# The value convolution and the low weight parts on GpSimd, and a reciprocal and square root in place of a logarithm and exponential, in the first projection stage of a two-block kernel

## What is computed

```python
r, k, v, wd, ad, gd = cols                       # columns of the projection x @ w_in
r, k, v = split(conv_fn(concatenate([r, k, v])), 3)   # depthwise 3x3 on the grid, 1x3 in the context
kk = heads(k * k_k)
kk = kk / maximum(sqrt(sum(kk * kk, per head)), 1e-12)
for d in range(2):
    w = -softplus(-(w0[d] + tanh(wl) @ w2[d])) - 0.5
    a_flat = sigmoid(a0[d] + al @ a2[d])
    kd = heads(k * (1.0 + (a_flat - 1.0) * k_a))
    bonus.append(sum(rh * kd * r_k, per head) * vh)
```

## Time and profile before

| | before |
|---|---|
| median of 3 runs | 5515.27 us (5512.98 to 5518.95) |
| the profiled execution | 5518.95 us, of which 5517.2 us from first to last instruction |
| granted TensorE clock, mean | 0.860 |
| busy: PE, DVE, ACT, POOL | 4372.5, 2100.7, 1445.7, 863.7 us |
| first and last product of the stage `front` | 231 and 885 us |
| steps of one half | 231 to 534 us, then 577 to 885 us |

### The profile page before, as it was taken

The page is one execution under the profiler, slowest core; times in us unless marked ns, Lnnn a source line. Parts: engine busy times, 40 slices in busy tenths (PEclk is TensorE's granted clock), DMA queues, the critical chain, the costliest instruction groups (busy, mean ns, idle before and its releaser), DMA issues. The chain is left out here.

```text
span 5517.2 us, 85137 instructions
## 1 busy us (share of the span) xinstructions
PE 4372.5 (79%) x33087; PEld 2998.3 (54%) x33088; DVE 2100.7 (38%) x3440; ACT 1445.7 (26%) x2777; POOL 863.7 (16%) x836
## 2 busy tenths in 40 slices
PE   4698896777768857369999999999607999884569
PEld 0497886767667753334444444444305777663434
DVE  0288685555533341321111111111266663235600
ACT  0276564222200000202333333333102221342200
POOL 2100001333300000041111111111122333001100
PEclk9799898989955558589999999999858999996689
DMA  3444444212032323228588887322463223204331
GB/s 137 123 147 152 128 145 132 67 52 65 23 73 57 67 74 137 70 79 292 205 311 299 323 300 278 135 94 92 155 236 70 77 77 95 81 20 98 67 122 64
DMA packets 615451, 720.50 MB, mean 131 GB/s; under 512 B 89380, under 2 KB 495652, under 8 KB 615172
## 3 DMA queue, kind: packets, MB, share of 16 engines
q1 hardware_dynamic: 554184, 544.39, 31.8%
q0 software_dynamic: 39344, 135.94, 6.6%
q10 hardware_dynamic: 21648, 36.18, 1.8%
HBM read 542.44 MB, written 173.97 MB: 130 GB/s over the span
## 5 line engine op out<-in xcount | busy, mean ns | idle before, releaser
L2337 PE MATMUL routed_p_gu<-routed_wgu,routed_xT 128*128 x2048 | 903.2, 594 | 7.9 <-SPq L2261 7.5
L2337 PEld LDWEIGHTS routed_p_gu<-routed_wgu,routed_xT 128*128 128x128 f32 x2048 | 381.0, 191 | 438.2 <-issue 438.2
L2319 PE MATMUL routed_p_y<-routed_wd,routed_hT 128*128 x1024 | 460.5, 593 | 1.4 <-DVE routed_y L2386 1.4
L2357 ACT ACTIVATE routed_xT<-routed_p_x,moe_bias,moe_scale 128x128 f32<-128x128 f32 x1032 | 374.1, 468 | 99.2 <-PE routed_p_x L2308 99.2
L2398 DVE TENSOR_TENSOR routed_hid<-routed_sg,routed_p_gu 128x256 f32<-128x256 f32 x128 | 53.9, 421 | 873.9 <-ACT routed_sg L2368 873.9
L1850 PE MATMUL out_ps<-out_w,out_a 128*128 128x512 f32 x768 | 334.2, 599 | 58.4 <-DMA out_x<-h 36.4
L626 PE MATMUL front_ps<-front_a_high,front_w_high 128*128 128x320 f32 (+1 forms) x1120 | 364.2, 325 | 16.7 <-DVE front_w_low L861 13.6
L626 PE MATMUL front_ps<-front_a_high,front_w_low 128*128 128x320 f32 (+1 forms) x1120 | 355.5, 317 | 0.0
L626 PE MATMUL front_ps<-front_a_low,front_w_high 128*128 128x320 f32 (+1 forms) x1120 | 355.3, 317 | 0.0
L2319 PEld LDWEIGHTS routed_p_y<-routed_wd,routed_hT 128*128 128x128 f32 x1024 | 194.9, 190 | 245.7 <-issue 245.7
L2284 POOL DMA_INDIRECT results<-routed_y,routed_yidx x128 | 124.9, 976 | 1169.8 <-DVE routed_idx L2377 871.8
(11 more groups left out here) (509 smaller groups left out, 7431.8 us busy)
## 6 DMA issues: line engine op xcount, KB each, us to landing
routed_wgu<-in_exp_w_gate_dram SPq DMA_DIRECT2D x64, 1024.0 KB, 6.9
routed_wgu<-in_exp_w_up_dram SPq DMA_DIRECT2D x64, 1024.0 KB, 11.9
routed_wd<-in_exp_w_down_dram SPq DMA_DIRECT2D x64, 1024.0 KB, 13.9
front_wt<-in_w_in_dram SPq DMA_DIRECT2D x70, 512.0 KB, 4.3
sum_part<-results SPq DMA_DIRECT2D x8, 4096.0 KB, 13.7
mod_w<-in_w_mod_dram SPq DMA_DIRECT2D x12, 2048.0 KB, 7.7
pre_wt<-in_w_in_dram SPq DMA_DIRECT2D x44, 512.0 KB, 3.9
proj<-pre_xv SPq DMA_DIRECT2D x16, 512.0 KB, 2.6
```

Of the source, the lines that this page charges most:

```text
L2319: op = nc.tensor.matmul(p_y[:, h, :], hT[:, k, :], wd[:, bass.ds(e % WS, 1), k, h * BANK:(h + 1) * BANK], start=(k == 0), stop=(k == MT - 1))
L2337: op = nc.tensor.matmul(p_gu[:, :], xT[:, b % 2, k, :], wgu[:, bass.ds(e % WS, 1), k, :, :], start=(k == 0), stop=(k == KD - 1))
L2357: op = nc.scalar.activation(xT[:, b % 2, k, :], p_x[:, k // 4, (k % 4) * P:(k % 4 + 1) * P], ACT.Identity, bias=bias[:, 0, k:k + 1], scale ...
```

## The change

POOL takes over `low` (all 70 low parts) and the whole value convolution, tap by tap: one multiply by a scalar into `term` and one add, with a drain ahead of each. The taps of one unit are cut over the six steps v to g (2, 2, 1, 2, 1, 2 taps for n < 4 and 1, 2, 1, 2, 1, 1 for n >= 4), each time behind `low(s + 2)`. The centre taps of k and r and the affine part of kd move from ACT to DVE, that of v to POOL. The logarithm and exponential become a reciprocal on DVE and a square root on ACT. The product of kk with the root, and `keys(n, 0)`, move from step q to step v on DVE.

```diff
@@ -589,10 +587,46 @@
 
         @block.gpsimd
         def _(pool):
-            for t, (src, idx) in enumerate(sources[0] + sources[1]):
-                size = src.shape[0]
-                pool.wait_ge(scaled, t + 1)
-                nc.gpsimd.tensor_tensor(yb[0:size, t % 2], yb[0:size, t % 2], row_shift[idx][0:size], ALU.add).then_inc(y_made, 1)
+            def low(s):
+                pool.wait_ge(w_rounded, s + 1)
+                nc.gpsimd.tensor_tensor(w_low[:, s % 2], wt[:, s % 2], w_high[:, s % 2], ALU.subtract).then_inc(w_split, 1)
+
+            def value_taps(n, first, last):
+
+                t, dst = taps[:, n % QT, 2, :], b("vc")
+                steps_of = around(n)
+                if first == 0:
+                    pool.wait_ge(bonus_made, n)
+                    pool.wait_ge(v_sent, 16 * n)
+                    nc.gpsimd.tensor_scalar(dst, raw[:, 2, offset(n):offset(n) + HALF], t[:, 4:5], None, ALU.mult)
+                for where, src, k in steps_of[first:last]:
+                    pool.drain()
+                    nc.gpsimd.tensor_scalar(where(b("term")), src(raw[:, 2]), t[:, k:k + 1], None, ALU.mult)
+                    pool.drain()
+                    nc.gpsimd.tensor_tensor(where(dst), where(dst), where(b("term")), ALU.add)
+                if last >= len(steps_of):
+                    pool.drain()
+                    pool.sem_inc(v_made, 1)
+
+            for s in range(N):
+                if s in (0, PER):
+                    for j, (src, idx) in enumerate(sources[s // PER]):
+                        t, size = s // PER * NT + j, src.shape[0]
+                        pool.wait_ge(scaled, t + 1)
+                        nc.gpsimd.tensor_tensor(yb[0:size, t % 2], yb[0:size, t % 2], row_shift[idx][0:size], ALU.add).then_inc(y_made, 1)
+                        if s == 0 and j in (1, 2):
+                            low(j - 1)
+                if s == 0:
+                    pool.wait_ge(once, 16 * ONCE)
+                if s + 2 < N:
+                    pool.wait_ge(mm_done, s + 1)
+                    low(s + 2)
+                for lag in range(6):
+                    n = at(s, "v", lag)
+                    if n is not None:
+                        pool.wait_ge(evicted, s - lag + 1)
+                        cuts = (0, 2, 4, 5, 7, 8, 10) if n < QT else (0, 1, 3, 4, 6, 7, 8)
+                        value_taps(n, cuts[lag], cuts[lag + 1])
...
@@ -709,13 +743,6 @@
                 act.wait_ge(aux_ready, 7 * n + j + 1)
                 return aux[:, (7 * n + j) % 2, :, 0:HALF // 2]
 
-            def keys(n, d):
-                if n:
-                    act.wait_ge(fac_made[d], n)
-                act.drain()
-                nc.scalar.activation(b(("kd0", "kd1")[d]), b(("sa0", "sa1")[d]), ACT.Identity, scale=cols[:, n % QT, KA:KA + 1],
-                                     bias=cols[:, n % QT, OMKA:OMKA + 1]).then_inc(kd_made[d], 1)
-
             def factors(n, d):
                 act.wait_ge(logs[d], n + 1)
                 inc, exc, neg = (("cm0", "ex0", "ng0"), ("sw1", "ex1", "ng1"))[d]
@@ -756,19 +783,7 @@
                 elif kind in ("k", "r", "v"):
                     if n:
                         act.wait_ge({"k": k_made, "r": r_made, "v": v_made}[kind], n)
-                    j, dst = {"r": (0, "rc"), "k": (1, "kc"), "v": (2, "vc")}[kind]
-                    nc.scalar.copy(two(raw[:, j, :]), wide).then_inc(evicted, 1)
-                    if n:
-                        if kind == "r":
-                            act.wait_ge(fac_made[1], n)
-                        elif kind == "k":
-                            act.wait_ge(prod_made, n)
-                        else:
-                            act.wait_ge(bonus_made, n)
-                            act.wait_ge(v_sent, 16 * n)
-                    act.drain()
-                    nc.scalar.activation(b(dst), raw[:, j, offset(n):offset(n) + HALF], ACT.Copy, scale=taps[:, i, j, 4:5])\
-                        .then_inc(centred[j], 1)
+                    nc.scalar.copy(two(raw[:, {"r": 0, "k": 1, "v": 2}[kind], :]), wide).then_inc(evicted, 1)
                 elif kind == "q":
                     if n:
                         act.wait_ge(h_made[1], n)
@@ -793,14 +808,11 @@
                     if n:
                         act.wait_ge(fac_sent[0], 80 * n)
                     nc.scalar.activation(two(b("sa0")), ready, ACT.Sigmoid, bias=cols[:, i, A0:A0 + 1]).then_inc(aux_act, 1)
-                    keys(n, 0)
                     act.wait_ge(kk_made, n + 1)
                     nc.scalar.activation(b("sq"), b("kk"), ACT.Square).then_inc(kk_squared, 1)
                 elif kind == "v":
-                    act.wait_ge(aux_dve, 2 * n + 1)
-                    nc.scalar.activation(b("sq"), b("sq"), ACT.Ln)
-                    act.drain()
-                    nc.scalar.activation(b("sq"), b("sq"), ACT.Exp, scale=-0.5).then_inc(kk_rooted, 1)
+                    act.wait_ge(kk_inverse, n + 1)
+                    nc.scalar.activation(b("sq"), b("sq"), ACT.Sqrt).then_inc(kk_rooted, 1)
                 elif kind == "q":
                     ready = take(n, 3)
                     if n:
@@ -808,7 +820,6 @@
                     nc.scalar.activation(two(b("sw1")), ready, ACT.Sigmoid, bias=cols[:, i, W0 + 1:W0 + 2]).then_inc(aux_act, 1)
                 elif kind == "ff":
                     nc.scalar.activation(two(b("sa1")), take(n, 4), ACT.Sigmoid, bias=cols[:, i, A0 + 1:A0 + 2]).then_inc(aux_act, 1)
-                    keys(n, 1)
                     factors(n, 0)
                 elif kind == "fb":
                     for d in range(2):
@@ -845,8 +856,6 @@
                             dve.wait_ge(turned, t - 1)
                         nc.vector.scalar_tensor_tensor(yb[0:size, t % 2], xb[0:size, t % 2], part[:, 2:3], row_scale[idx][0:size],
                                                        ALU.mult, ALU.mult).then_inc(scaled, 1)
-                    if half == 0 and j in (1, 2):
-                        low(j - 1)
                     if j >= 1:
                         size = sources[half][j - 1][0].shape[0]
                         dve.wait_ge(high_made, t)
@@ -856,13 +865,9 @@
                             op = nc.vector.tensor_tensor(cells[0][:, h], turns[:, h], cells[1][:, h], ALU.subtract)
                         op.then_inc(low_made, 1)
 
-            def low(s):
-                dve.wait_ge(w_rounded, s + 1)
-                nc.vector.tensor_tensor(w_low[:, s % 2], wt[:, s % 2], w_high[:, s % 2], ALU.subtract).then_inc(w_split, 1)
-
             def convolution(n, j, dst):
                 t = taps[:, n % QT, j, :]
-                dve.wait_ge(centred[j], n + 1)
+                nc.vector.tensor_scalar(dst, raw[:, j, offset(n):offset(n) + HALF], t[:, 4:5], None, ALU.mult)
                 for where, src, k in around(n):
                     dve.drain()
                     op = nc.vector.scalar_tensor_tensor(where(dst), src(raw[:, j]), t[:, k:k + 1], where(dst), ALU.mult, ALU.add)
@@ -877,9 +882,12 @@
                 return by(ap, size)[:, :, k:k + 1].broadcast_to([P, n_chunks, size])
 
             def keys(n, d):
+                i = n % QT
                 kd, sa = b(("kd0", "kd1")[d]), b(("sa0", "sa1")[d])
-                dve.wait_ge(kd_made[d], n + 1)
+                dve.wait_ge(aux_act, 5 * n + (2 if d == 0 else 4))
+                nc.vector.tensor_scalar(kd, sa, cols[:, i, KA:KA + 1], cols[:, i, OMKA:OMKA + 1], ALU.mult, ALU.add)
                 nc.vector.tensor_tensor(sa, sa, b("kk"), ALU.mult)
+                dve.drain()
                 nc.vector.tensor_tensor(kd, kd, b("kc"), ALU.mult)
 
             def factors(n, d):
@@ -933,8 +941,6 @@
                     nc.vector.tensor_tensor(lb[:, :, 2, :], lb[:, :, 0, :], lb[:, :, 1, :], ALU.subtract).then_inc(lb_diff, 1)
                     dve.wait_ge(lb_sig, 1)
                     nc.vector.tensor_scalar(lb[:, :, 3, :], lb[:, :, 2, :], -1.0, 1.0, ALU.mult, ALU.add)
-                if s + 2 < N:
-                    low(s + 2)
                 n = at(s, "g", 1)
                 if n is not None:
                     dve.wait_ge(aux_ready, 7 * n + 7)
@@ -948,25 +954,26 @@
                     gla_factors(n, 1)
                 n = at(s, "k")
                 if n is not None:
+                    dve.wait_ge(evicted, s + 1)
                     convolution(n, 1, b("kc")).then_inc(k_made, 1)
                     dve.drain()
                     nc.vector.tensor_scalar(b("kk"), b("kc"), cols[:, n % QT, KKC:KKC + 1], None, ALU.mult).then_inc(kk_made, 1)
                 n = at(s, "r")
                 if n is not None:
+                    dve.wait_ge(evicted, s + 1)
                     convolution(n, 0, b("rc")).then_inc(r_made, 1)
                 n = at(s, "v")
                 if n is not None:
                     dve.wait_ge(aux_ready, 7 * n + 3)
```

(5 more changed lines are left out.)

6 lines of the change are left out of this document (2 added, 4 removed).

## The result

| | before | changed |
|---|---|---|
| median | 5516.11 us (5512.98 to 5518.95, 4 runs) | 5600.28 us (5595.21 to 5611.8, 4 runs) |
| the profiled execution | 5518.95 us | 5587.35 us |
| first and last instruction apart | 5517.2 us | 5585.6 us |
| busy: PE, DVE, ACT, POOL | 4372.5, 2100.7, 1445.7, 863.7 us | 4387.9, 2204.6, 1394.8, 1326.7 us |

The changed kernel is slower: 1.0155 times the time before, with a 95% interval of 1.0138 to 1.0174, so about 85 us. The predicted 5576 us is 24 us too low. The time lies in the stated range (5510 to 5640), but above the forecast's own (5555 to 5597).

What follows compares the result with a forecast made beforehand. PE sets the pace until the DVE, ACT and POOL ring becomes slower. Eight units at 6.4 (51), between halves +8, start +1, end +1: 61 us onto 5518.95, 5580, less 3.7 for the median: 5576; own range 5555 to 5597, whole 5510 to 5640.

Steps and rivals of the forecast that it cites:

- no change: Rival: fewer DVE and POOL instructions meet than counted, PE stays the bound; 5510 us; chance 0.18.
- faster: Rival: POOL not held at `v_made` in step g, which comes at 401.9; -12 us, 5503 us; chance 0.07.
- The ring: DVE, ACT and POOL followed through one unit: steps sum to 8.0 us, less PE's 1.61 us slack, 6.4 a unit.
- (d): From the maximum to the root: 3.7 us becomes 5.7 with the reciprocal, +2.0 us; ACT waits for it.
- (e): From the root to ACT's L731: four held DVE instructions +3.3 us, ACT's affine part gone -0.9, together +2.4.
- (b): Step g: POOL's low part and last two taps give `v_made` at 405.4; L944 behind it +0.8 us.
- (c): L944 to L960: two low parts go (-2.4), two centre taps come (+1.1), two POOL low parts hold (+4.1): +2.8 us.
- the turn between the halves: SP's gain load waits for unit 3's `v_made`, 543.0 against 534.99: +8 us.
- It is nearest to the copy: POOL's multiply by a scalar priced near its one-input copy, 1.04 us for 1024 elements; 3996 elements 4.1 us a unit.
- POOL dearer: Rival: POOL's multiplies cost what its adds cost, 6.5 us more a unit (second half 7.7); 57 us more, 5633; chance 0.20.
- All that lies beside PE's products and is worth nothing by itself: Work leaving DVE and ACT gains nothing alone; DVE's unit work becomes 49.1 us (second half 51.6), ACT loses 6.4.
- The exclusion rule: DVE and POOL on SBUF wait for each other's whole instruction, 0.28 us saved per POOL instruction; DVE's reciprocal exempt.

## Why the prediction was right, and which of its steps failed

**Direction, place and range held.** PE went from the bound to waiting. It waits for low parts, as the forecast had it, but for none of ACT's evictions, which the forecast named too: its other new wait is for ACT's square ahead of the sums over heads. The forecast saw that square queue behind `v_made` and k, but gave PE's wait for it no term. Rival "no change" fell: with both jobs on POOL each unit is 10 us longer. Rival "faster" needed `v_made` 5.1 us behind the start of step g's low part, and has it 8.6 behind (487.26 to 495.89), so that DVE waits 3.84 us ahead of 496.03.

**The ring, by its steps**, one unit (before from the earlier trace rows and the unit that starts at 355.67; changed from 442.00):

| stretch | before | changed | measured | forecast |
|---|---|---|---|---|
| maximum to the low part of step g (d, e, less slack) | 355.67 to 396.76, 41.1 | 442.00 to 487.26, 45.3 | +4.2 | +2.8 |
| to the bonus (b) | to 404.63, 7.9 | to 496.03, 8.8 | +0.9 | +0.8 |
| to the next maximum (c) | to 424.49, 19.9 | to 520.45, 24.4 | +4.6 | +2.8 |
| sum | 68.8 | 78.45 | +9.6 | +6.4 |

(c) was mis-sized by one instruction. Three of POOL's low parts stand in the way, not two: DVE's products at 496.99 and 499.90 are held 1.4 and 2.2 us, and the r taps take 8.73 us instead of the 6.36 of their kind in the earlier trace rows, 2.4 more, with the low part of 513.76 beside them. That is 6.0, less 2.4 for two low parts gone, plus 1.1 for two centre taps: +4.6. (d) was right: the root on ACT starts 5.10 us behind the maximum (447.10) instead of 2.94, so +2.2 for a forecast of 2.0. That leaves 2.0 of the first line for (e) less the slack, which were put at 2.4 less 1.6, so 0.8: 1.2 too little.

**The sum.** From the starts of the eight maxima:

| stretch | before | changed | measured | forecast |
|---|---|---|---|---|
| start of the stage to the first maximum | 284.36 | 281.28 | -3.1 | +1 |
| three intervals, first half | 208.9 | 239.2 | +30.2 | 3 x 6.4 |
| over the turn between the halves | 136.0 | 148.0 | +12.0 | +8, and a unit's share |
| three intervals, second half | 219.0 | 253.9 | +34.9 | 3 x 6.4 |
| last maximum to the next stage | 68.7 | 77.2 | +8.5 | +1, and a unit's share |

The terms give 82.5 us against the forecast's 61. The turn itself was right (+9.0 for +8), the start had the wrong sign, and the end's +1 can't be told from the share of a unit in that row. The unit was mis-sized, at 10.1 (first half) and 11.6 us (second half) for 6.4, outside the 4 to 9 that the forecast allowed for it. The whole time lies in the stated range only because that reaches to the rivals.

**The clock was left out.** The forecast takes PE's products at full clock, without a word on it. They took 19.3 us more for the same instructions, nearly the 24 us that the median is off; but part of it lies beside other waits, so this alone isn't shown to be the miss.

**POOL's work: the price was wrong.** "It is nearest to the copy" put 0.65 us on a multiply by a scalar of 640 elements. It takes 1.89 alone. (The forecast's last sentence has 4 us a unit for each 0.4 ns an element; 3996 elements make that 1.6.) POOL's 54.2 us of busy time a unit stand against the 31.8 that were forecast. This is the premise of the rival "POOL dearer"; its conclusion, 57 us more "all in full shared time", was wrong as well, since a multiply holds DVE for only 0.5 to 0.9 us. The two misses work against one another, by luck: the rival's premise held, and the forecast's amount was the nearer one.

**"All that lies beside PE's products and is worth nothing by itself": this step failed.** The forecast costed what is moved between ACT and DVE by how much work each engine has in all, 49.1 of 68.8 us. Moves and reciprocal with nothing on POOL cost 55 us, the moves 17, the reciprocal 38 without POOL and 22 with it. The work is in the wrong place: the reciprocal and the moved product and `keys` all stand in step v on DVE, ahead of the low part of step q, or ahead of ACT's root, which stands ahead of the eviction of q. These are steps (d) and (e) of the forecast's own ring, followed there only with the low parts off DVE. In the changed kernel ACT's wait for the reciprocal is 81.1 us where it was 26.9.

**The exclusion rule.** The pairs at 477.60 to 499.90 above show DVE held through a POOL low part, as the earlier trace rows had it, and the reciprocal was not held (4.15 us in all eight). For POOL's multiply the trace differs: 0.5 us held of 1.96. The Trainium skill ("SBUF — State Buffer", section "SBUF: two separate sides") says that the one that starts first gets the pair of ports for its whole instruction. By that rule 30 scaled adds beside eight multiplies would have taken 24.3 + 8 x 1.96 = 40 us; they took 28.28. The measurement decides. The Trainium skill ("GPSIMD Engine Reference", section "4.1 Engine selection") has GpSimd about twice slower for two inputs and at about line rate for one; here one input with a scalar is dearer on POOL than two (1.89 against 1.53 us).

**Logarithm and exponential.** Their costs of +38 and +22 for the replacement say that the two table loads on ACT were the better bargain, since ACT had time beside PE's products and DVE in that place had none.

**What stays open.** How (e) splits among the instructions held, and how much of the 82.5 us the lower clock makes by itself. Low parts and value convolution on POOL together cost 31 us more than the sum of the two without the rest of the change, and 64 us more with it (85 - 24 - 52 + 55). Where PE loses it is shown above; that POOL's own queue makes `v_made` and the low parts late together is in part argued. The timeline speaks for it: from 453.90 to 485 us POOL has no idle time over 0.2 us, and the low parts at 460.47 and 477.60 start right behind a tap, so each is late by taps and holds DVE later. The kernel with earlier value taps fits: `v_made` came in time and the low parts later still (56.4 us of PE's waits for 43.6). The value convolution alone on POOL with the low parts on DVE, logarithm kept and the moves made, was not run either.

## What to carry to other kernels

Cost a moved operation by what stands behind it in its new queue, not by how full that engine is: DVE had 10 us to spare in each unit and 4 us of reciprocal ahead of one low part still cost 38 us in all. Count the clock with each wait of PE: the same products took 19.3 us longer here. Test the parts of a change alone and together, in both directions: the same move gained 31 us and lost 22 here, and two moves of 7 and 22 us made 60. Before work goes to POOL, measure there the very instruction, alone and beside DVE, since neither its duration nor what it holds follows from its neighbours.

## What the runs showed of the hardware

POOL's multiply by a scalar of one operand is dearer than its add of two (1.89 against 1.53 us for 640 elements; 0.93 for 255), yet it holds DVE less (0.5 us beside scaled adds, 0.92 beside multiplies, against 1.24 for the add). DVE's reciprocal is slow, 4.15 us for 640 elements or 6.5 ns each, and runs beside POOL's multiply and add with no loss to either (POOL's 1.88 and 1.53 us there are its times alone). The shortest form in itself, the product with a broadcast tap (1.35 us), made the kernel 31 us slower than the longest. POOL's multiply waits for DVE at times: 2.86 us for 378 elements beside a scan, 1.24 alone. Waits of PE of 5.4 and 6.8 us were followed by a granted clock of 0.50 until 515 and 380 us, in which a matmul of 320 columns lasts 0.47 us instead of 0.31.
